# First self-attention: attention weights turned by 32x32 block transposes and gathering DMAs instead of TensorE transposes, and ScalarE's rounding of weights moved in its queue

## The chip, the cores and the metric

The kernel runs on one core of one Trainium2 chip, in one launch. The metric is the device time of that core in microseconds. The core has four computing engines, each with a queue of its own that runs in order: TensorE (PE in the views; its weight loads are PEld), VectorE (DVE), ScalarE (ACT) and GpSimd (POOL). SyncE (SP) issues the DMAs. The engines wait for each other on counted semaphores.

## The reference

Two blocks of two layers each run on a sequence of 512 tokens with 1024 features. The change lies in the first block's attention, in both of its layers:

```python
# first block, per layer; h = rms_norm(x); p = h @ w_in
q = apply_rope(rms_norm(q, q_g)); k = apply_rope(rms_norm(k, k_g))   # 8 heads of 64
score = sum_h relu(iq_h . ik) * iw_h            # an index score for each query and key
_, idx = lax.top_k(score masked causally, 128)  # 128 keys for each query
s = q . k_sel * HEAD_DIM ** -0.5                # causal, only the selected keys
p = softmax(s); o = p @ v_sel
y_b = (o * silu(gate)) @ w_out_attn
merged = g0 * y_conv + g1 * y_b + g2 * y_pool;  x = x + merged @ w_o
```

The rest of the first block (a short convolution and a pooling branch) and the second block (attention, a Hyena convolution, gated linear attention, cross-attention, a feed-forward part) are projections of the same kind with work of their own between them.

## The kernel before

**Units and queues.** `order_of_work` writes one list of units (`plan`). Every engine walks the same list and does its part of each unit, so the list sets the order of all queues. In the first block three lists (main: attention; sel: the top-k bias; side: the other branches) are merged by a string of digits, `PICKS["one0"]` and `PICKS["one"]`, written out by hand: each digit names the list that gives the next unit.

**Projections.** Most units are projections ("weight units" below: `q`, `k`, `agate`, `gate`, `by`, `hy`, `xk` and so on). A weight block travels: SP loads it into one of three raw buffers (`WRAW`); ACT rounds it into one of three buffers `WSP` (the high part, `next_halves`, L1350); POOL subtracts to get the rest (the low part, L1732); PE multiplies with three matmuls for each 128 features (L942 to L944). A full unit is 24 matmuls of 512 columns, a `by` unit of the first block 12. ACT calls `next_halves` at the head of a weight unit, before that unit's own work, for the block two ahead; the call waits for the matmuls of the block that used the same `WSP` buffer, three before it.

**Attention of the first block.** Heads go in pairs (`c` = 0 to 3, `hh` = 0, 1) and queries in four tiles of 128 (`i`). Only keys up to the tile's end are used, so tile `i` has 128(i+1) keys.

- `sc`: PE writes the scores into banks S0 and S1 (L1111). DVE adds the bias, takes the maximum and writes the scores to `PA` in SBUF (L2110), ACT takes the exponential in place with its sum (L1538).
- `nrm`: DVE inverts the sum, ACT scales `PA` (L1549).
- `tr`: PE turns the weights, one 128x128 transpose for each block of keys (L1007 on `PA`), into banks T0 and T1. DVE copies head 0 out (L2148), ACT head 1 (L1557), into `PTA`.
- `pv`: PE multiplies `PTA` with the values (L1148) into bank O. `atty` and `split` gate and round the result.
- `qss`, `kbc`: PE sums squares for the norms of `q` and `k` (L1082, sixteen instructions with 2 columns each) and turns the factors.

**The second block already turns its weights otherwise:** DVE transposes blocks of 32x32 (`STREAM_TRANSPOSE`, L2132, `BLK<-PB`), and eight DMAs a half (L2740, `PTB<-BLK`) bring blocks of the same key residue together on the partitions.

**Names that the steps touch.** `fspec` (L1198) and `tokx` (L1581, `HX<-B`) are units of the Hyena part; `park` evicts a gate to `HYT` and to DRAM. `msq` (L1649) squares the memory for the cross-attention; `go` is the gate of the linear attention (`GS<-B`); `xk` projects the memory (`MN`).

Of the kernel before, what the change touches and what calls it, by code (L numbers as in the profile page):

```python
# [23 lines left out]
        "1211211222112211120001102121112222011121211112212212100000200000000000020002002000002000000000000020"  # L24
        "020000000200000200020002000002000"
# [3 lines left out]
        "2212121211121212121121200000112121212112121112112121221212000002000000002000002000020000020000000000"  # L29
        "00020020000000200002002000002000002000"  # L30
# [329 lines left out]
def order_of_work(steps):  # L360
# [41 lines left out]
    def block_one(l):  # L402
# [34 lines left out]
        main += qk(0)  # L437
        for c in range(4):
            nxt = qk(c + 1) if c < 3 else []
            for i in range(4):  # L440
                main.append(Unit("sc", "a", l, c, i, s=True))
                main += nxt[:2]
                nxt = nxt[2:]
                if i:
                    main.append(Unit("tr", "a", l, c, i - 1, t=True))
                main.append(Unit("nrm", "a", l, c, i))
            main += nxt
            main.append(proj("agate", l, c, src=H, w=[(*A, "agate", c)]))
            main.append(Unit("tr", "a", l, c, 3, t=True))
            main.append(Unit("pv", "a", l, c, o=True))  # L450
            main += [Unit("atty", l, c), Unit("split", "YB", A, c)]
# [203 lines left out]
def program(nc, ins, place, out, steps=8):  # L655
    ctx = ExitStack()
    with ctx:
# [22 lines left out]
        PA, PTA, RXA, GA = at(45, "PA", 4), at(49, "PTA", 8), at(57, "RXA", 4), at(62, "GA", 3)  # L680
# [246 lines left out]
        def tensor(e):  # L927
# [85 lines left out]
            for u in plan:  # L1013
# [81 lines left out]
                elif k == "sc":  # L1095
# [7 lines left out]
                    for hh in range(2):  # L1103
                        half = slice(64 * hh, 64 * hh + 64)
                        if ab == "a":
                            b = take((S0, S1)[hh], dve_done, ("smax", ab, l, c, i, hh))
# [5 lines left out]
                elif k == "tr":  # L1112
                    ab, l, c, i = a
                    nk = i + 1
                    for hh in range(2):
                        b = take((T0, T1)[hh], (dve_done, act_done)[hh], ("pt", ab, l, c, i, hh))
                        w.wait_ge(act_done, ("nrm", ab, l, c, i, hh))
                        p = PA[:, 2 * (i % 2) + hh, :]
                        turn(b, [p[:, 128 * j:128 * j + 128] for j in range(nk)], nk, ("tr", ab, l, c, i, hh))
# [18 lines left out]
                elif k == "pv":  # L1138
                    ab, l, c = a
                    b = take(O, dve_done, ("lo", "YB", ("a", l), c))  # L1140
                    w.wait_ge(dve_done, ("pt", ab, l, c, 3, 0))
                    w.wait_ge(act_done, ("pt", ab, l, c, 3, 1))
                    w.wait_ge(act_done, ("tok", "vtok", l, 3))
                    for j in range(4):
                        q0 = 128 * j
                        for hh in range(2):
                            v = VA4[:, j, 128 * c + 64 * hh:128 * c + 64 * hh + 64]
                            x = e.matmul(b[64 * hh:64 * hh + 64, q0:512], v, PTA[:, 4 * hh + j, q0:512], start=j == 0, stop=j == 3)  # L1148
# [190 lines left out]
        def scalar(e):  # L1339
# [40 lines left out]
            for u in plan:  # L1380
                k, a = u.kind, u.a
                if own[-1] != act_done.n:
                    w.value(act_done.sem, own[-1])
                    own.append(act_done.n)
                for g in range(len(u.w)):
                    if u.w0 + g:
                        next_halves(u.w0 + g + NSP - 1)
                if k == "nadd":
# [137 lines left out]
                elif k == "sc":  # L1526
                    ab, l, c, i = a
                    n = 128 * (i + 1) if ab == "a" else 512
                    m = SM[:, 6 + i, :]
                    load_table(ACT.Exp)  # L1530
                    w.wait_ge(dve_done, ("neg", ab, l, c, i))
                    if ab == "b" and (c or i > 1):
                        back = (c, i - 2) if i > 1 else (c - 1, i + 2)
                        w.wait_ge(dve_done, ("blocks", l, *back, 1))
                    for hh in range(2):
                        p = (PA if ab == "a" else PB)[:, 2 * (i % 2) + hh, 0:n]
                        s = p if ab == "a" else banks[score_bank(ab, i, hh)][:, :]
# [5 lines left out]
                elif k == "nrm":  # L1543
                    ab, l, c, i = a
                    n = 128 * (i + 1)
                    w.wait_ge(dve_done, ("rsum", ab, l, c, i))
                    for hh in range(2):
                        p = PA[:, 2 * (i % 2) + hh, 0:n]
                        e.activation(p, p, ACT.Copy, scale=SM[:, 6 + i, 6 + hh:7 + hh]).then_inc(  # L1549
                            *act_done.up(("nrm", ab, l, c, i, hh)))  # L1550
                elif k == "tr":
                    ab, l, c, i = a
                    nk = i + 1
                    if i == 0 and c:
                        w.wait_ge(mm_done, ("pv", ab, l, c - 1))
                    w.wait_ge(mm_done, ("tr", ab, l, c, i, 1))
                    e.activation(PTA[:, 4:4 + nk, 128 * i:128 * i + 128],  # L1557
                                 banks[T1][:, 0:128 * nk].rearrange("p (k q) -> p k q", q=128), ACT.Copy).then_inc(
                        *act_done.up(("pt", ab, l, c, i, 1)))
# [245 lines left out]
        def vector(e):  # L1805
# [80 lines left out]
            for u in plan:  # L1886
# [206 lines left out]
                elif k == "sc":  # L2093
                    ab, l, c, i = a
                    n = 128 * (i + 1) if ab == "a" else 512
                    m, q2 = SM[:, 6 + i, :], SM[:, 4 + c % 2, 2 * i:2 * i + 2]
                    if ab == "a":
# [3 lines left out]
                        if c or i > 1:  # L2101
                            back = (c, i - 2) if i > 1 else (c - 1, i + 2)
                            w.wait_ge(mm_done, ("tr", ab, l, *back, 1))
# [38 lines left out]
                elif k == "tr":  # L2142
                    ab, l, c, i = a
                    nk = i + 1
                    if i == 0 and c:
                        w.wait_ge(mm_done, ("pv", ab, l, c - 1))
                    w.wait_ge(mm_done, ("tr", ab, l, c, i, 0))
# [409 lines left out]
        def sync(e):  # L2557
# [58 lines left out]
            for n_unit, u in enumerate(plan):  # L2616
# [405 lines left out]
```

## Time and profile before

| | us |
|---|---|
| median of 3 runs | 3255.43 (3254.47 to 3259.03) |
| profiled execution | 3252.9, its span 3250.9 |
| PE busy | 3223.4 |
| DVE, ACT, POOL busy | 1613.1, 1292.0, 1570.8 |

The span runs from the first instruction to the last. A busy PE is not PE at its peak: ends of matmuls are modelled and overlap the next start, so what an instruction costs is read from the distance between starts. `PEclk` is the TensorE clock that was granted, as a share of 2.4 GHz (0.50 is 1.2 GHz).

### The profile page before, as it was taken

How to read it: one execution, taken by the hardware profiler on the slowest of the kernel's cores; microseconds unless marked ns; L12 is line 12 of the kernel's file. 1: busy time of each engine (PE TensorE's matmuls, PEld its weight loads, DVE VectorE, ACT ScalarE, POOL GpSimd, SP SyncE). 2: the span in 40 equal slices, each digit the busy share in tenths (PEclk: the TensorE clock that was granted, in tenths of full speed). 3: DMA queues.
4: the chain of work that ended last, by engine and by line, in shares of the span. 5: the costliest groups of instructions: out<-in, count | busy, mean ns of one | idle time of the engine just before them, and what ended most of it. 6: DMA issues, size and time to landing. Idle time of an engine off the chain costs nothing.

```text
span 3250.9 us, 40100 instructions
## 1 busy us (share of the span) xinstructions
PE 3223.4 (99%) x15156; PEld 2547.6 (78%) x15156; DVE 1613.1 (50%) x2736; ACT 1292.0 (40%) x1984; POOL 1570.8 (48%) x1224
## 2 busy tenths in 40 slices
PE   9999999999999999999999999999999999999999
PEld 7788778787877767767788888887676788888887
DVE  4566433546543678864555321227887455442020
ACT  4343643334464322454446322232235544642231
POOL 4554334545434563334463565646333446446473
PEclk9999999999999999999999999999999999999999
DMA  4323224323223523452353433334236235334332
GB/s 158 98 84 97 75 88 147 120 94 92 81 84 91 184 98 101 142 145 81 112 182 98 130 118 97 102 122 139 91 119 166 77 112 187 118 117 123 97 91 97
DMA packets 145976, 370.16 MB, mean 114 GB/s; under 512 B 18670, under 2 KB 35630, under 8 KB 145784
## 3 DMA queue, kind: packets, MB, share of 16 engines
q1 hardware_dynamic: 145784, 367.60, 37.0%
q8 instruction: 120, 1.97, 0.2%
q14 instruction: 72, 0.59, 0.1%
HBM read 316.02 MB, written 25.30 MB: 105 GB/s over the span
## 4 chain that ended last, share of the span: by engine, by line
PE 93%; DVE 4%; ACT 2%; issue 1%; POOL 1%; DMA 0%; SPq 0%; DVEq 0%; ACTq 0%
PE B L942 27%; PE B L944 27%; PE B L943 27%; PE B L1007 1%; PE B L1111 1%; PE B L1134 1%; PE B L1167 1%; PE B L1209 1%; PE B L1217 1%; PE B L1198 1%; POOL WSP L1732 1%; PE B L1082 1%; PE B L1073 1%; PE B L1148 1%; PE B L1203 0%
## 5 line engine op out<-in xcount | busy, mean ns | idle before, releaser
L1732 POOL TENSOR_TENSOR WSP<-WRAW,WSP 128x512 fp32r<-128x512 f32 x1036 | 1359.0, 1333 | 1469.9 <-ACT WSP L1350 1469.4
L942 PE MATMUL B<-H,WSP 128*128 128x512 f32 x2496 | 993.0, 398 | 7.7 <-POOL WSP L1732 7.7
L944 PE MATMUL B<-H,WSP 128*128 128x512 f32 x2496 | 972.6, 390 | 0.0
L943 PE MATMUL B<-H,WSP 128*128 128x512 f32 x2496 | 971.9, 389 | 0.0
L1350 ACT ACTIVATE WSP<-WRAW 128x1024 fp32r<-128x1024 f32 (+1 forms) x567 | 555.8, 984 | 669.3 <-PE B L944 528.7
L942 PEld LDWEIGHTS B<-H,WSP 128*128 128x128 f32 x2496 | 468.8, 188 | 127.6 <-issue 25.3
L943 PEld LDWEIGHTS B<-H,WSP 128*128 128x128 f32 x2496 | 469.0, 188 | 100.9 <-issue 6.9
L944 PEld LDWEIGHTS B<-H,WSP 128*128 128x128 f32 x2496 | 468.5, 188 | 99.0
L1815 DVE TENSOR_TENSOR B<-B,RN 128x512 f32<-128x512 f32 x194 | 134.8, 697 | 392.1 <-PE B L944 375.8
L942 PE MATMUL B<-YM,WSP 128*128 128x512 f32 x512 | 199.5, 390 | 0.0
L944 PE MATMUL B<-YM,WSP 128*128 128x512 f32 x512 | 199.2, 389 | 0.0
L943 PE MATMUL B<-YM,WSP 128*128 128x512 f32 x512 | 199.2, 389 | 0.0
L2554 DVE TENSOR_TENSOR XN<-B,XN 128x512 f32<-128x512 f32 x32 | 22.1, 692 | 295.6 <-PE B L944 295.6
L2546 DVE SCALAR_TENSOR_TENSOR MR<-B,RN 128x512 f32<-128x512 f32 x64 | 44.3, 692 | 249.4 <-PE B L944 249.3
L1803 POOL TENSOR_TENSOR MR<-MR 128x512 f32<-128x512 f32 x64 | 88.6, 1385 | 91.3 <-DVE MR L2546 91.3
L942 PEld LDWEIGHTS B<-YM,WSP 128*128 128x128 f32 x512 | 96.1, 188 | 21.4 <-DVE XN L2554 1.6
L944 PEld LDWEIGHTS B<-YM,WSP 128*128 128x128 f32 x512 | 96.1, 188 | 20.0
L943 PEld LDWEIGHTS B<-YM,WSP 128*128 128x128 f32 x512 | 96.1, 188 | 19.9
L1370 ACT ACTIVATE GA<-B 128x512 f32<-128x512 f32 x48 | 28.7, 598 | 200.9 <-DVE B L1815 200.9
L942 PE MATMUL B<-YAC,WSP 128*128 128x512 f32 x256 | 103.5, 404 | 0.0
L943 PE MATMUL B<-YAC,WSP 128*128 128x512 f32 x256 | 101.1, 395 | 0.0
L944 PE MATMUL B<-YAC,WSP 128*128 128x512 f32 x256 | 100.9, 394 | 0.0
(451 smaller groups left out, 4806.8 us busy)
## 6 DMA issues: line engine op xcount, KB each, us to landing
WRAW<-in_wb SPq DMA_DIRECT2D x318, 512.0 KB, 3.7
WRAW<-in_wa SPq DMA_DIRECT2D x153, 512.0 KB, 3.7
PTB<-BLK SPq DMA_DIRECT2D x128, 128.0 KB, 2.7
WRAW<-in_wa SPq DMA_DIRECT2D x50, 256.0 KB, 2.6
WRAW<-in_wb SPq DMA_DIRECT2D x48, 256.0 KB, 2.6
parked<-HYT SPq DMA_DIRECT2D x24, 256.0 KB, 2.1
QA<-RXA SPq DMA_DIRECT2D x64, 64.0 KB, 2.0
xs<-PA SPq DMA_DIRECT2D x16, 256.0 KB, 4.4
```

What stands on the lines that cost most here:

```text
L942: e.matmul(o, L[0], R[0], start=first, stop=False)
L943: e.matmul(o, L[0], R[1], start=False, stop=False)
L944: return e.matmul(o, L[1], R[0], start=False, stop=last)
L1007: x = e.transpose(b[:, 128 * i:128 * i + 128], src[i], eye)
L1073: e.matmul(b[:, 0:n], QA[half, c % 2, 128 * i:128 * i + 128], KA[half, 1, 0:n], start=True, stop=True).then_inc(*mm_done.up(("idx", l, c, ...
L1082: x = e.matmul(b[:, 8 * n + 2 * i:8 * n + 2 * i + 2], sq[:, 128 * i:128 * i + 128], pair[:, ::64], start=True, stop=True)
L1111: e.matmul(b[:, 0:n], q, kk, start=True, stop=True).then_inc(*mm_done.up(("sc", ab, l, c, i, hh)))
L1350: e.activation(WSP[:, i % NSP, 0, 0:n * cols], WRAW[:, i % NRAW, 0:n * cols], ACT.Copy).then_inc(*hi_done.up(i))
L1732: x = e.tensor_tensor(WSP[:, i % NSP, 1, c:c + CUT], WRAW[:, i % NRAW, c:c + CUT], WSP[:, i % NSP, 0, c:c + CUT].bitcast(fp32), ALU.subtract)
L1803: e.tensor_tensor(t, t, t, ALU.mult).then_inc(*pool_done.up((k, *a)))
L1815: e.tensor_tensor(pj(u)[:, :], pj(u)[:, :], RN[:, :], ALU.mult).then_inc(*dve_done.up(("scaled", u.pj)))
L2546: e.scalar_tensor_tensor(MR[:, c % 4, :], pj(u)[:, :], 0.0, RN[:, :], ALU.max, ALU.mult).then_inc(*dve_done.up(("pj", u.pj), (k, *a)))
```

## The change

The `tr` units of the first block go. ACT now writes the exponentials in blocks of 32 keys into `PA`, reading the scores from the PSUM bank in a permuted order, so that key 128j+4k+b lies in block b; DVE transposes these 32x32 blocks in place (`ablocks`); SP gathers them with eight DMAs for each half of the queries (`agather`) into `PTA`; `pv` reads `PTA` with strides. Scores of four tiles use four banks. The order around the attention is written anew, and both strings of digits with it (two of their lines are shown). Apart from that, in all stages, ACT's `next_halves` now stands right behind a weight unit's own work, for the block three ahead (not for `woa` units).

```diff
 PICKS = {
     "one0": (
-        "1211211222112211120001102121112222011121211112212212100000200000000000020002002000002000000000000020"
+        "1211211222112211120001100212111222201112121111221221210000000000000020000200000000000000000000200002"
...
-        for c in range(4):
-            nxt = qk(c + 1) if c < 3 else []
-            for i in range(4):
-                main.append(Unit("sc", "a", l, c, i, s=True))
-                main += nxt[:2]
-                nxt = nxt[2:]
-                if i:
-                    main.append(Unit("tr", "a", l, c, i - 1, t=True))
-                main.append(Unit("nrm", "a", l, c, i))
-            main += nxt
-            main.append(proj("agate", l, c, src=H, w=[(*A, "agate", c)]))
-            main.append(Unit("tr", "a", l, c, 3, t=True))
-            main.append(Unit("pv", "a", l, c, o=True))
-            main += [Unit("atty", l, c), Unit("split", "YB", A, c)]
+        nxt = qk(1)
+        main += qk(0) + [sc(0, 0), *nxt[:2], nrm(0, 0), sc(0, 1), *nxt[2:4], turned(0, 0), nrm(0, 1), sc(0, 2), *nxt[4:], turned(0, 1),
+                         Unit("agather", l, 0, 0), nrm(0, 2), sc(0, 3), turned(0, 2), nrm(0, 3), turned(0, 3), Unit("agather", l, 0, 1)]
+        for c in range(4):
+            nxt = qk(c + 2) if c < 2 else []
+            if c:
+                main += [Unit("agather", l, c, 0), sc(c, 2), sc(c, 3), nrm(c, 2), turned(c, 2), nrm(c, 3), turned(c, 3),
+                         Unit("agather", l, c, 1)]
+            main += nxt[:2] + [proj("agate", l, c, src=H, w=[(*A, "agate", c)])]
+            if c < 3:
+                main += [sc(c + 1, 0), sc(c + 1, 1), nrm(c + 1, 0), nrm(c + 1, 1), *nxt[2:], turned(c + 1, 0), turned(c + 1, 1)]
+            main += [Unit("pv", "a", l, c, o=True), Unit("atty", l, c), Unit("split", "YB", A, c)]
...
-            return (S0, S1)[hh] if ab == "a" else (S0, S1, T0, T1)[(2 * i + hh) % 4]
+            return (S0, S1, T0, T1)[(2 * i + hh) % 4]
+        def query_half(t, h, hh):
+            return t[:, 2 + 2 * hh:4 + 2 * hh, :].rearrange("p s x -> p (s x)") if h else t[:, hh, :]
+        def weights_tile(i, hh):
+            t = query_half(PA, i // 2, hh).rearrange("p (b j i k) -> p i b j k", b=4, i=2, k=32)
+            return t[:, i % 2, :, 0:i + 1, :]
...
-                    for j in range(4):
-                        q0 = 128 * j
-                        for hh in range(2):
-                            v = VA4[:, j, 128 * c + 64 * hh:128 * c + 64 * hh + 64]
-                            x = e.matmul(b[64 * hh:64 * hh + 64, q0:512], v, PTA[:, 4 * hh + j, q0:512], start=j == 0, stop=j == 3)
+                    for h in range(2):
+                        for j in range(2 * h + 2):
+                            i0 = max(2 * h, j)
+                            for hh in range(2):
+                                v = VA4[:, j, 128 * c + 64 * hh:128 * c + 64 * hh + 64]
+                                p = query_half(PTA, h, hh).rearrange("p (r j q) -> p j r q", r=4, j=2 * h + 2)[:, j, :, 32 * (i0 - 2 * h):64]
+                                o = b[64 * hh:64 * hh + 64, :].rearrange("p (i r q) -> p r i q", i=4, r=4)[:, :, i0:2 * h + 2, :]
+                                x = e.matmul(o, v, p, start=j == 0, stop=j == 2 * h + 1)
...
-            for u in plan:
+            begun = None
+            for behind, u in zip([None] + plan, plan):
...
+                if behind and behind.w and behind.kind != "woa":
+                    next_halves(behind.w0 + len(behind.w) + NSP - 1)
                 for g in range(len(u.w)):
-                    if u.w0 + g:
+                    if g or begun and begun.kind == "woa":
                         next_halves(u.w0 + g + NSP - 1)
+                begun = u if u.w else begun
...
-                            x = e.tensor_tensor_reduce(out=PA[:, 2 * (i % 2) + hh, 0:n], in0=b[:, 0:n], in1=bias, scale=1.0, scalar=NEG,
+                            x = e.tensor_tensor_reduce(out=b[:, 0:n], in0=b[:, 0:n], in1=bias, scale=1.0, scalar=NEG,
                                                        op0=ALU.add, op1=ALU.max, accum_out=m[:, hh:hh + 1])
...
-                    e.tensor_copy(PTA[:, 0:nk, 128 * i:128 * i + 128],
-                                  banks[T0][:, 0:128 * nk].rearrange("p (k q) -> p k q", q=128)).then_inc(
-                        *dve_done.up(("pt", ab, l, c, i, 0)))
+                elif k == "ablocks":
+                    l, c, i = a
+                    for hh in range(2):
+                        p = weights_tile(i, hh)
+                        w.wait_ge(act_done, ("nrm", "a", l, c, i, hh))
+                        e.transpose(p, p).then_inc(*dve_done.up(("ablocks", l, c, i, hh)))
...
+                elif k == "agather":
+                    l, c, half = a
+                    next_raw(coming[n_unit] + NRAW + half)
+                    if half == 0 and c:
+                        w.wait_ge(mm_done, ("pv", "a", l, c - 1))
+                    w.wait_ge(dve_done, ("ablocks", l, c, 2 * half + 1, 1))
+                    for hh in range(2):
+                        for q in range(4):
+                            n = 128 + 128 * half
+                            e.dma_start(query_half(PTA, half, hh)[:, n * q:n * q + n], query_half(PA, half, hh)[32 * q:32 * q + 32]).then_inc(
+                                *gathered[half].up((k, *a)))
```

The first place is PE's queue in the first layer, around the product of head pair 1 (`pv`, `B<-PTA,VA`): the rows in it other than projections. Before:

```order
L1148 MATMUL B<-PTA,VA 64x512 [waits s_act_done,s_dve_done]
L1148 MATMUL B<-PTA,VA 64x512
L1148 MATMUL B<-PTA,VA 64x384 x2
L1148 MATMUL B<-PTA,VA 64x256 x2
L1148 MATMUL B<-PTA,VA 64x128 x2
L1111 MATMUL B<-KA,QA 128x128 x2
...
L1111 MATMUL B<-KA,QA 128x256 [waits s_dve_done] x2
L1082 MATMUL B<-CST,RXA 128x2 [waits s_act_done]
L1082 MATMUL B<-CST,RXA 128x2 x3
...
L1007 MATMUL B<-CST,PA 128x128 [waits s_act_done] x2
L1111 MATMUL B<-KA,QA 128x384 [waits s_dve_done] x2
```

And in the changed kernel:

```order
L1158 MATMUL B<-PTA,VA 64x4x2x32 [waits s_gathered1,s_gathered0]
L1158 MATMUL B<-PTA,VA 64x4x2x32
L1158 MATMUL B<-PTA,VA 64x128 x2
L1158 MATMUL B<-PTA,VA 64x4x2x32 x6
L1158 MATMUL B<-PTA,VA 64x128 x2
L1126 MATMUL B<-KA,QA 128x384 x2
L1126 MATMUL B<-KA,QA 128x512 x2
...
L1126 MATMUL B<-KA,QA 128x128 [waits s_act_done] x2
L1126 MATMUL B<-KA,QA 128x256 [waits s_act_done] x2
L1097 MATMUL B<-CST,RXA 128x2 [waits s_act_done]
L1097 MATMUL B<-CST,RXA 128x2 x3
```

The transposes of `PA` are gone, two `sc` units stand side by side, the product has twelve matmuls in place of eight over the same columns, and waits for the gathers. Between the scores of tiles 2 and 3 and the product that needs their gathers stand five projections: four full ones and a `by`, or three full ones and two `by`.

The second place is ACT's queue in the second block, at the change from the linear attention to the memory (`MACC`, `KSQ` are `msq`; `WSP<-WRAW` is a rounding). Before:

```order
L1639 ACTIVATE SM<-SM,EPSC 128x8 [waits s_dve_done]
L1649 ACTIVATE MACC<-MT 128x512 [waits s_act_done]
L1649 ACTIVATE KSQ<-MT 128x512
L1649 ACTIVATE KSQ<-MT 128x512 [waits s_dve_done] x2
L1350 ACTIVATE WSP<-WRAW 128x1024 [waits s_raw1,s_act_done]
L1364 ACT_TABLE_LOAD
L1364 ACTIVATE GS<-B 128x512 [waits s_dve_done]
L1350 ACTIVATE WSP<-WRAW 128x1024 [waits s_mm_done,s_raw2,s_act_done]
```

And in the changed kernel:

```order
L1656 ACTIVATE KSQ<-MT 128x512
L1656 ACTIVATE KSQ<-MT 128x512 [waits s_dve_done] x2
L1374 ACT_TABLE_LOAD [waits s_dve_done]
L1374 ACTIVATE GS<-B 128x512 [waits s_act_done]
L1360 ACTIVATE WSP<-WRAW 128x1024 [waits s_mm_done,s_raw2,s_act_done]
L1383 ACTIVATE KSQ<-B 128x256 [waits s_mm_done]
```

The rounding with `s_raw1` has left this place: it now stands further up, ahead of the squares of `gout` and of all of `msplit` and `msq`. And the table load ahead of `GS<-B` now carries the wait for DVE that the activation behind it carried before; in the whole program 25 table loads do so, where 4 did.

## Rows read from the trace of the kernel before

**Rows 1.** The page, busy time of each engine

```profile
PE 3223.4 (99%) x15156; PEld 2547.6 (78%) x15156; DVE 1613.1 (50%) x2736; ACT 1292.0 (40%) x1984; POOL 1570.8 (48%) x1224
```

**Rows 2.** The page, chain that ended last

```profile
PE 93%; DVE 4%; ACT 2%; issue 1%; POOL 1%; DMA 0%; SPq 0%; DVEq 0%; ACTq 0%
```

**Rows 3.** All waits of PE: waited for, total us, times, longest

```profile
PE B L942 <- POOL WSP L1732: 14.7, 9, 5.5
PE B L1007 <- ACT PA L1549: 1.8, 2, 1.0
PE B L1007 <- DVE SM L2110: 1.7, 2, 0.9
```

**Rows 4.** Groups of PE, forms apart: the transposes of PA

```profile
L1007 PE MATMUL B<-CST,PA 128*128 128x128 f32 x160 | 24.5, 280 | 3.7 <-ACT PA L1549 1.8 <-DVE SM L2110 1.7 <-DVE MS L2166 0.2
```

**Rows 5.** Timeline of PE: start us, us, instruction; eight transposes

```profile
323.42 0.39 PE L944 MATMUL B<-H,WSP 128*128 128x512 f32 x1
323.65 1.14 PE L1007 MATMUL B<-CST,PA 128*128 128x128 f32 x8
324.54 0.47 PE L942 MATMUL B<-H,WSP 128*128 128x512 f32 x1
325.08 0.40 PE L944 MATMUL B<-H,WSP 128*128 128x512 f32 x1
```

**Rows 6.** Timeline of PE: one product pv, and what follows

```profile
330.20 2.37 PE L1148 MATMUL B<-PTA,VA 128*64 128x512 f32 x16
332.51 0.49 PE L1111 MATMUL B<-KA,QA 64*128 64x128 f32 x4
```

**Rows 7.** Windows of PE: busy (instructions), PEclk, DMA share, GB/s

```profile
346.80:350.30 3.50, 3.50 (x10) 0.51 0.50 95
940.70:944.20 3.50, 3.50 (x9) 0.52 0.71 193
1596.00:1603.00 7.00, 3.66 (x17) 0.51 0.15 40
```

**Rows 8.** Timeline of PE: three waits for a low part

```profile
1413.63 0.47 PE L942 MATMUL B<-H,WSP 128*128 128x512 f32 x1 [1.65 <-POOL WSP L1732]
...
1512.89 0.47 PE L942 MATMUL B<-H,WSP 128*128 128x512 f32 x1 [1.17 <-POOL WSP L1732]
...
1599.34 0.55 PE L942 MATMUL B<-MN,WSP 128*128 128x256 f32 x1 [5.46 <-POOL WSP L1732]
```

**Rows 9.** Timeline of ACT ahead of two of these waits

```profile
1407.77 1.28 ACT L1519 ACT_TABLE_LOAD   x1
...
1409.23 1.05 ACT L1350 ACTIVATE WSP<-WRAW 128x1024 fp32r<-128x1024 f32 x1
...
1595.60 1.04 ACT L1350 ACTIVATE WSP<-WRAW 128x1024 fp32r<-128x1024 f32 x1
...
1598.44 1.05 ACT L1350 ACTIVATE WSP<-WRAW 128x1024 fp32r<-128x1024 f32 x1
```

**Rows 10.** PA and BLK by instruction: duration ns min/median/max

```profile
L1538 ACT ACTIVATE PA<-PA,SM x64: 477/648/817, 185.0 to 987.1; 128x128 f32<-128x128 f32 x16, 128x256 f32<-128x256 f32 x16, 128x384 f32<-128x384 f32 x16, 128x512 f32<-128x512 f32 x16
L1549 ACT ACTIVATE PA<-PA,SM x64: 386/555/725, 196.7 to 989.0; 128x128 f32<-128x128 f32 x16, 128x256 f32<-128x256 f32 x16, 128x384 f32<-128x384 f32 x16, 128x512 f32<-128x512 f32 x16
...
L2740 SPq DMA_DIRECT2D PTB<-BLK x128: 543/607/1740, 1353.5 to 2516.6; - x128
L2132 DVE STREAM_TRANSPOSE BLK<-PB x64: 664/686/712, 1350.1 to 2511.4; 128x512 f32<-128x512 f32 x64
...
DMA to landing us min/median/max: 2.5/2.7/3.8
```

**Rows 11.** Timeline of ACT, then of PE, at the unit tokx

```profile
1208.43 0.60 ACT L1370 ACTIVATE HYT<-B 128x512 f32<-128x512 f32 x1 [3.56 <-DVE B L1815]
1209.07 2.06 ACT L1581 ACTIVATE HX<-B 128x512 f32<-128x512 f32 x4
...
1210.28 3.60 PE L1198 MATMUL B<-HR,DF 128*128 128x512 f32 x8
```

More of the change, by code:

```diff
@@ L28 @@
         "0200002002000202022000200220022002012200000110121020200011221212000011211121121122220202202102012121"
-        "2212121211121212121121200000112121212112121112112121221212000002000000002000002000020000020000000000"
-        "00020020000000200002002000002000002000"
+        "2212121211121212121121200000011212121211212111211212122121200000000000000200002000000000000000000002"
+        "0000200000000000000200202020000000000002222000"
     ),
@@ L679, in program @@
         BIAS, VA4, QA, KA = at(34, "BIAS", 3), at(37, "VA4", 4), at(41, "QA", 2), at(43, "KA", 2)
-        PA, PTA, RXA, GA = at(45, "PA", 4), at(49, "PTA", 8), at(57, "RXA", 4), at(62, "GA", 3)
+        PA, PTA, RXA, GA = at(45, "PA", 6), at(51, "PTA", 6), at(57, "RXA", 4), at(62, "GA", 3)
         HR, HY = (at(0, "HR0", 8), at(16, "HR1", 8)), at(16, "HY", 8)
@@ L1105, in tensor @@
                         if ab == "a":
-                            b = take((S0, S1)[hh], dve_done, ("smax", ab, l, c, i, hh))
+                            b = take(score_bank(ab, i, hh), act_done, ("exp", ab, l, c, i, hh))
                             q, kk = QA[half, c % 2, 128 * i:128 * i + 128], KA[half, c % 2, 0:n]
@@ L1111, in tensor @@
                         e.matmul(b[:, 0:n], q, kk, start=True, stop=True).then_inc(*mm_done.up(("sc", ab, l, c, i, hh)))
-                elif k == "tr":
-                    ab, l, c, i = a
-                    nk = i + 1
-                    for hh in range(2):
[L1116 to L1119, printed above, removed]
                 elif k == "pbc":
@@ L1140, in tensor @@
                     b = take(O, dve_done, ("lo", "YB", ("a", l), c))
-                    w.wait_ge(dve_done, ("pt", ab, l, c, 3, 0))
-                    w.wait_ge(act_done, ("pt", ab, l, c, 3, 1))
+                    for h in range(2):
+                        w.wait_ge(gathered[h], ("agather", l, c, h))
                     w.wait_ge(act_done, ("tok", "vtok", l, 3))
-                    for j in range(4):
-                        q0 = 128 * j
-                        for hh in range(2):
-                            v = VA4[:, j, 128 * c + 64 * hh:128 * c + 64 * hh + 64]
-                            x = e.matmul(b[64 * hh:64 * hh + 64, q0:512], v, PTA[:, 4 * hh + j, q0:512], start=j == 0, stop=j == 3)
+                    for h in range(2):
+                        for j in range(2 * h + 2):
[5 more added lines that the diff above has]
+                                x = e.matmul(o, v, p, start=j == 0, stop=j == 2 * h + 1)
                     x.then_inc(*mm_done.up(("pv", *a)))
@@ L1531, in scalar @@
                     w.wait_ge(dve_done, ("neg", ab, l, c, i))
+                    if ab == "a" and c:
+                        w.wait_ge(gathered[i // 2], ("agather", l, c - 1, i // 2))
                     if ab == "b" and (c or i > 1):
@@ L1535, in scalar @@
                     for hh in range(2):
-                        p = (PA if ab == "a" else PB)[:, 2 * (i % 2) + hh, 0:n]
-                        s = p if ab == "a" else banks[score_bank(ab, i, hh)][:, :]
+                        p = weights_tile(i, hh) if ab == "a" else PB[:, 2 * (i % 2) + hh, :]
+                        s = banks[score_bank(ab, i, hh)][:, :]
+                        if ab == "a":
+                            s = s[:, 0:128 * (i + 1)].rearrange("p (j k b) -> p b j k", k=32, b=4)
                         e.activation(p, s, ACT.Exp, bias=m[:, 2 + hh:3 + hh], scale=SM[:, 4 + c % 2, 2 * i + hh:2 * i + hh + 1],
@@ L1544, in scalar @@
                     ab, l, c, i = a
-                    n = 128 * (i + 1)
                     w.wait_ge(dve_done, ("rsum", ab, l, c, i))
                     for hh in range(2):
-                        p = PA[:, 2 * (i % 2) + hh, 0:n]
+                        p = weights_tile(i, hh)
                         e.activation(p, p, ACT.Copy, scale=SM[:, 6 + i, 6 + hh:7 + hh]).then_inc(
                             *act_done.up(("nrm", ab, l, c, i, hh)))
[L1551 to L1559, printed above, removed]
                 elif k in ("fm1", "fm2"):
@@ L2096, in vector @@
                     m, q2 = SM[:, 6 + i, :], SM[:, 4 + c % 2, 2 * i:2 * i + 2]
+                    if (ab, c, i) == ("a", 0, 0):
+                        for x in range(8 if l else 0):
+                            w.wait_ge(landed, ("xs", 1, x))
+                        for h, t in enumerate((PA[:, 0:2, :], PA[:, 2:6, :])):
+                            ahead = t.rearrange("p s x -> p (s x)").rearrange("p (n j x) -> p j n x", n=8, j=2 + 2 * h)
+                            e.memset(ahead[:, 1 + 2 * h, :, 0:32], 0.0).then_inc(*dve_done.up(("ahead", l, h)))
                     if ab == "a":
```

20 lines of the change are left out of this document (8 added, 12 removed).

## The prediction

> **What bounds the kernel now.** I read the page's busy line first: TensorE is busy for 3223.4 us of a span of 3250.9, the three other engines for half of theirs or less [rows 1]. The chain that ended last says the same: 93% of it is PE, and no other engine has more than 4% [rows 2]. So time moves only when PE's queue gets shorter, when PE waits less, or when its clock changes; work on DVE, ACT, POOL or SP counts only where PE waits for it. Next, PE's waits: nine of them, 14.7 us in all, are for the low part of a weight block, and four more, 1.8 and 1.7 us, are at the transposes of `PA` [rows 3]. The timeline shows three of the nine with their lengths, 1.65, 1.17 and 5.46 us [rows 8]. Last, windows over stretches where PE's work looked thin show PEclk at 0.51 and 0.52 in place of full speed [rows 7].
>
> **The transposes.** The change takes away 160 of them, 24.5 us busy [rows 4]. Busy time overstates them, as their ends overlap. In the timeline eight stand between 323.65 and the next full matmul at 324.54, which is 0.89 us; the matmul behind them then reaches its successor only 0.54 us later (two full ones stand 0.23 apart ahead of them) [rows 5]. Some of that is wait rather than work, so I take 0.09 of it: 0.98 us for eight, 0.12 each. 160 times that is 19. In other places a few overlap better, so I take **-18.5**; the ends are -17.5 and, by busy time, -24.5. With them go PE's waits for ACT's scaling and for DVE at these instructions, **-3.5** [rows 3].
>
> **The product.** `pv` had 16 matmuls (eight in each of two halves of the array), 2.31 us from its start to the next instruction [rows 6]. It now has 24, over the same columns. Small matmuls cost nearly by their columns, so I take **0**. The upper bound from this side is one transpose for each of the 64 added instructions, 64 x 0.12 = +8. The other end is that a write in runs of 32 columns, strided over the bank, is slower: if it took twice as long, 8 x 2.3 = +18. No row of before has such a write, so this end is a rival below. The Trainium skill, "SBUF — State Buffer", section "Door 1: The DMA port swizzle", says that any non-contiguous PSUM access pattern significantly slows down matmuls; by it the sum below would lose up to those 18 us. No row before tests it; I give it a small chance, because the runs are 32 columns long and only their starts are strided.
>
> **What stands in for the transposes.** DVE: 64 block transposes of at most 0.69 us, less 32 copies. ACT: 32 copies less. SP: 128 more issues of 0.61 us each, 78 us in all [rows 10]. None is near PE's 99%. What matters is when `PTA` arrives. From the last scores of tile 3, one pair of tiles needs four exponentials of at most 0.82 us, four scalings of 0.73, four block transposes of 0.69, and DVE's reductions, for the first of which I take a transpose's 0.7 as an estimate: 3.3 + 2.9 + 2.8 + 0.7 = 9.7. Then eight issues of 0.61 (4.9) and a landing of 2.7: 17.3 us [rows 10]. The cover is the five projections between: a full unit is 24 matmuls of 0.227, 5.4 us (the step is that of [rows 5]), a `by` half, 2.7. Three full and two `by` give 21.8, four full and one `by` 24.5. So the gathers land 4 to 7 us ahead of `pv`: cost **0**. The slack is thin in this respect: ACT's queue now has a rounding (1.05 us) [rows 9] right behind each unit, ahead of exponentials, and where that rounding waits for its raw buffer, everything of the chain stands behind it. A landing can take 3.8 us, an issue 1.7 [rows 10]. SP issues two weight loads ahead of each set of gathers, so the raw buffers are filled first.
>
> **The clock.** Two stretches of 3.5 us run at half clock, each in the first block behind a stretch of thin work (scores, `qss`, transposes) [rows 7]. With the transposes gone PE comes to full columns sooner. If both go, each gives half its length, 1.7: **-3.4**. If `sc`, `sc` and `qss`, now side by side, thin the stretch as much, nothing.
>
> **Roundings moved.** The wait at 1413.63 follows a rounding that started at 1409.23, late because a table load and other work stood ahead of it [rows 8, 9]. Behind the unit that frees the slot it starts some microseconds earlier, so this 1.65 goes, and so does its like in the second layer (one of the remaining six of the nine, taken as long): -3.3. The wait of 1.17 at 1512.89 goes likewise: -1.2. The one of 5.46 us has two roundings ahead of it, 1595.60 and 1598.44 [rows 9]. The first moves far up, ahead of `msq`; the second now stands behind the gate `GS`, whose table load (1.28) waits for DVE. So the wait does not vanish: I take 2.5 off it, and half a microsecond off the half-clock stretch 1596 to 1603 [rows 7]: -3.0. Together **-7.5**; ends 0 and, if all 14.7 go and 3.5 of slow clock, -18.
>
> **What the move costs.** At `tokx` ACT's queue has `HYT<-B`, then four copies `HX<-B` that free banks for `fspec`, which starts 1.2 us behind the copies' start [rows 11]. Now the table load waits for DVE, so its 1.28 no longer hides in the 3.56 of idle time ahead of `HYT` [rows 9, 11], and a rounding of 1.05 stands ahead of the copies: they end 2.3 us later, at about 1213.4. `fspec` needs its next bank half-way, near 1212.1, and the third copy rather than the fourth: about 1 us of wait in each layer, **+2**. Ends 0 and 2 x 2.3 = +4.6.
>
> **Sum.** -18.5 - 3.5 + 0 - 3.4 - 7.5 + 2 = -30.9. The profiled execution took 3252.9, its span of 3250.9 and 2.0 around it, so after the change 3222.0. The median of the runs shown is 2.5 above the profiled one: 3224.5, and I write **3225**.
>
> **Rivals.** What follows are medians, 3255.4 plus each sum; 0.2% of it, 6.5 us, is about what a measurement of this kernel can tell from no change.
>
> *A, the forecast:* transposes, their waits, the slow stretches and half of the low-part waits go. 3218 to 3230.
>
> *B, the transposes alone:* -22, with clock and roundings giving nothing. The waits for POOL only change places, since ACT has as much to do as before at the same points and the string of digits puts units elsewhere. For it: the first of the two roundings at 1595.60 was early enough, and still PE waited [rows 8, 9]. 3233.
>
> *C, the strided product:* as A, but `pv` at double time, +18: 3243. For it: nothing in the rows; against it: the columns are the same and their runs long.
>
> *D, everything goes:* all 14.7 of the low-part waits, the half clock behind them, and no new wait at `fspec`: -18.5 - 3.5 - 3.4 - 18 = -43.4: 3212.
>
> *E, slower, the gathers arrive late:* the chain of 17.3 us becomes longer than its cover. It decides at 21.8 us for two head pairs and 24.5 for the other two. The place is the wait of `pv` for `gathered`. To eat the gain of 31 in eight products, each must wait 3.9 us; to be slower by 0.2%, 4.7, so a chain of 27 to 29 us. That takes ACT's queue held for 9 to 11 us in every pair, for example by a rounding that waits for a raw buffer not yet loaded. Then the time is 3262 and more, 3270 with the clock falling after such waits as it did after the 5.46 us one [rows 7, 8].
>
> *F, no change:* a part of E, 2 to 4 us a product, on average: 3249 to 3262.
>
> **How the numbers follow.** A 0.55; B 0.18; C 0.07; D 0.08; F 0.05; E 0.07. Likeliest is A, so 3225; its own range is 3218 to 3230. The range that holds 8 in 10 takes in B with its spread (-22 against the +4.6 and +8 of the bounds gives 3246 at the far end, most of it below 3240) and the edge of D: 3213 to 3240, leaving out the far half of D, C, and E and F. Faster by over 0.2% means below 3249: A, B, C, D, 0.88. Within 0.2%: F, 0.05. Slower: E, 0.07.
>
> **What would show it.** Transposes: no PE row on `PA`, PE's instruction count down by 160 less 64, busy time down by some 20. Product: eight groups of 24 at 2.3 us from start to next instruction; C shows as 4 us or more. Gathers: PE's waits for `PTB`-like landings on `PTA` of 0 to 1 us; E shows as several microseconds at each `pv`, with ACT or SP ahead of it in the chain. Clock: windows over the stretches of `sc`, `sc`, `qss` and the 4 us behind them, at 1.0 if right. Roundings: no wait of over 1 us for a low part near the memory of the convolution in either layer, about 3 us left at the first matmul on `MN`. New cost: a wait of PE for ACT inside `fspec`, near 1 us. The prediction is wrong by more than its range if waits stand at `pv`, if the clock falls in new places, or if the new order makes PE wait for scores or banks that the old one did not.

## The result, and the profile after

The changed kernel takes 3335.26 us (median of 4 runs, 3327.0 to 3339.2), against 3254.95 for the kernel before (4 runs, 3253.15 to 3259.03). The ratio is 1.0242, with a 95% interval of 1.0219 to 1.0264: 80 us slower, where 31 faster was forecast. The profiled run is the fastest of the four, 3327.0 with a span of 3325.2. One run of the kernel before, beside three of the experiments below, took 5153.48 us at a mean granted clock of 0.584, and is left out everywhere.

The page's busy line answers to [rows 1]:

```profile
PE 3235.3 (97%) x15060; PEld 2551.1 (77%) x15060; DVE 1672.7 (50%) x2772; ACT 1272.9 (38%) x1948; POOL 1592.2 (48%) x1224
```

PE issues 96 instructions fewer (160 transposes less, 64 matmuls more) and is nevertheless busy for 11.9 us longer. What PE is not busy has gone from 27.5 us (3250.9 less 3223.4) to 89.9. So five sixths of the 74.3 us by which the span has grown are waits. The rest is PE's busy time, which rose although PE has less to do: its mean granted clock is 0.990 in place of 0.998. By my estimate that costs some 26 us (0.008 of 3235.3), and the transposes that are gone hide about half of it. PE's waits by what was waited for (us in total, times, longest) answer to [rows 3]:

```profile
PE B L957 <- POOL WSP L1739: 25.2, 19, 3.2
PE B L1022 <- DVE RXA L1847: 23.5, 5, 6.9
PE B L957 <- DVE H L1905: 8.1, 7, 1.4
PE B L1097 <- ACT SM L1538: 6.9, 2, 3.5
PE B L1208 <- ACT HV L1588: 4.7, 2, 2.5
PE B L1263 <- ACT ES L1635: 4.6, 2, 2.3
PE B L1022 <- ACT GS L1374: 2.2, 1, 2.2
...
PE B L1208 <- ACT HX L1588: 1.3, 2, 0.7
```

No wait stands at the product `pv` (L1158) and none for a gather. Apart from some of the waits for the low part, only the second row lies in the new attention, and what PE waits for there is not the turned weights but `RXA`, the factor for the norm of `k`. The waits for `H`, `SM`, `HV`, `ES` and `GS` lie in parts of the program whose units did not change; only ACT's roundings moved there. The waits for the low part have grown from nine to nineteen.

ACT's own waits ahead of its roundings have changed as well. For raw blocks it stood 121.2 us in 45 waits before (53.4 and 67.8 us in these two rows); now it is 241.3 us in 72:

```profile
  DMA WRAW<-in_wa: 137.7, 35
  DMA WRAW<-in_wb: 103.6, 37
```

The timeline of PE shows one wait in the attention, and three at the norm behind the first layer:

```profile
354.06 1.09 PE L1022 MATMUL B<-CST,RXA 128*128 128x128 f32 x4 [6.60 <-DVE RXA L1847]
...
571.14 0.47 PE L957 MATMUL B<-H,WSP 128*128 128x512 f32 x1 [2.13 <-POOL WSP L1739]
...
576.70 0.50 PE L957 MATMUL B<-H,WSP 128*128 128x512 f32 x1 [1.23 <-DVE H L1905]
...
579.04 0.50 PE L957 MATMUL B<-H,WSP 128*128 128x512 f32 x1 [1.37 <-DVE H L1905]
```

Windows over three stretches (PE busy and its instructions, PEclk, DMA share, GB/s) answer to [rows 7]. The wait for `RXA` begins in the first window, at 347.5, still at full speed, and ends in the second; another lies in the third. In these two PEclk is 0.66, a mean of part at 0.5 and part at full speed:

```profile
340.00:350.00 10.00, 7.47 (x42) 1.00 0.53 178
350.00:360.00 10.00, 5.94 (x20) 0.66 0.14 52
390.00:400.00 10.00, 4.55 (x13) 0.66 0.19 52
```

**Why RXA is late.** Around 345 us ACT stands at a rounding, and its work for the attention stands behind it:

```profile
340.02 0.60 ACT L1374 ACTIVATE GA<-B 128x512 f32<-128x512 f32 x1 [2.44 <-DVE B L1822]
345.52 1.06 ACT L1360 ACTIVATE WSP<-WRAW 128x1024 fp32r<-128x1024 f32 x1 [4.90 <-DMA WRAW<-in_wa]
346.60 1.28 ACT L1367 ACT_TABLE_LOAD   x1
...
348.00 0.44 ACT L1555 ACTIVATE PA<-B,SM 128x128 f32<-128x128 f32 x1
...
351.46 1.28 ACT L1533 ACT_TABLE_LOAD   x1
352.75 0.27 ACT L1533 ACTIVATE SM<-B,EPSC 128x16 f32<-128x16 f32 x1
```

`GA<-B` is the own work of `agate`. Directly behind it stands the moved rounding, which waits 4.90 us for its raw block. PE had ended the scores for the exponentials at 340.04, and VectorE its part of them at 341.66. The `SM<-B` at the end feeds `RXA`. SP's queue says why the raw block was late:

```profile
330.72 5.13 SPq L2744 DMA_DIRECT2D PTA<-PA  x8
335.96 2.49 SPq L2570 DMA_DIRECT2D QA<-RXA  x4
338.55 2.91 SPq L2570 DMA_DIRECT2D KA<-RXA  x4
341.50 1.55 SPq L2584 DMA_DIRECT2D WRAW<-in_wa  x3
```

Eight gathers and eight rotations are issued one behind the other, and only then the next three raw blocks. The first of them is asked for at 341.50, and the rounding starts 4.0 us later.

**Why the norms are late.** In the stretch in which the first block's result is normed, SP saves and loads tiles of the residual (`xs`, `PA`). ACT's queue and SP's, in the kernel after:

```profile
1114.42 1.06 ACT L1360 ACTIVATE WSP<-WRAW 128x1024 fp32r<-128x1024 f32 x1 [5.07 <-issue]
1115.39 0.70 ACT L1406 ACTIVATE H<-PA,PAR 128x512 fp32r<-128x512 f32 x1
...
1122.35 1.06 ACT L1360 ACTIVATE WSP<-WRAW 128x1024 fp32r<-128x1024 f32 x1 [5.74 <-issue]
```

```profile
1110.00 0.43 SPq L2584 DMA_DIRECT2D WRAW<-in_wa  x1
...
1117.43 0.32 SPq L2570 DMA_DIRECT2D PA<-xs  x1
1117.80 0.43 SPq L2584 DMA_DIRECT2D WRAW<-in_wa  x1
```

This is a ring: a raw block is asked for at 1110.00; its rounding starts 4.4 us later, at 1114.42; behind it ACT makes `H`; DVE's part of `H` ends at 1117.40; SP's load `PA<-xs` waited for that; behind it, at 1117.80, stands the next raw block, and its rounding comes at 1122.35. One turn is 7.8 to 7.9 us, where a full unit of PE takes 5.4. The timeline names no cause for these two roundings (it says "issue"). But one turn earlier, where a block was asked for at 1100.34 and its rounding started at 1104.77, it names the DMA of the raw block, and the distance from the ask to the rounding is the same 4.4 to 4.6 us each time. In the kernel before roundings stood as far behind their asks, but the same rounding came one tile of the norm later in ACT's order, so that SP's next load did not wait for work behind it; roundings came 5.2 to 5.8 us apart there.

### The profile page after: what moved, and what is told of

The parts are those of the page before. It is cut to its first block and busy times, and to the rows that moved or that the text cites. A ratio compares the mean times of both kernels' runs of the same rounds, so it can differ in the third digit from the quotient of the medians.

```text
span 3325.2 us, 40059 instructions
## 1 busy us (share of the span) xinstructions
PE 3235.3 (97%) x15060; PEld 2551.1 (77%) x15060; DVE 1672.7 (50%) x2772; ACT 1272.9 (38%) x1948; POOL 1592.2 (48%) x1224
## 5 line engine op out<-in xcount | busy, mean ns | idle before, releaser
L1739 POOL TENSOR_TENSOR WSP<-WRAW,WSP 128x512 fp32r<-128x512 f32 x1036 | 1402.1, 1375 | 1490.9 <-ACT WSP L1360 1490.2
L1810 POOL TENSOR_TENSOR MR<-MR 128x512 f32<-128x512 f32 x64 | 67.5, 1054 | 99.5 <-DVE MR L2553 97.7
```

The costliest lines, as they stand in the source:

```text
L1739: x = e.tensor_tensor(WSP[:, i % NSP, 1, c:c + CUT], WRAW[:, i % NRAW, c:c + CUT], WSP[:, i % NSP, 0, c:c + CUT].bitcast(fp32), ALU.subtract)
L1810: e.tensor_tensor(t, t, t, ALU.mult).then_inc(*pool_done.up((k, *a)))
```

## The experiments

The ratios are against runs of the kernel before beside each experiment; its medians there were 3254.12 (move_alone, attention_alone, early_asks), 3255.09 (hybrid, att_asks, hybrid_asks, before_four), 3257.34 (after_agate, asks_agate, move_asks) and 3257.25 us (twice).

**move_alone** is the kernel before with ACT's roundings moved and nothing else. **attention_alone** is the changed kernel with them back. Their difference from the one and the other kernel is this piece:

```diff
-                for g in range(len(u.w)):
-                    if u.w0 + g:
-                        next_halves(u.w0 + g + NSP - 1)
+                if behind and behind.w and behind.kind != "woa":
+                    next_halves(behind.w0 + len(behind.w) + NSP - 1)
+                for g in range(len(u.w)):
+                    if g or begun and begun.kind == "woa":
+                        next_halves(u.w0 + g + NSP - 1)
```

> The kernel before, with ScalarE's roundings moved behind the weight units and nothing else of the change. Theory 1 (the loss comes from the moved roundings: each now stands ahead of other ScalarE work and waits for a raw buffer that SP has not asked for in time): 3300 to 3330 us, with PE's new waits outside the attention, in the hyena, norm and memory stretches, as in the changed kernel. Theory 2 (the loss comes from the new attention, its gathers on SP's queue and what they push back): 3245 to 3260, as before or a little faster.

Measured: 3333.47 us, ratio 1.0244 (1.0226 to 1.0263). That is 3.5 us above the range of theory 1 and far from theory 2: the loss was even larger than theory 1 had it. PE's waits for `H`, `SM`, `ES` and `HV` are those of the changed kernel to within 0.5 us:

```profile
PE B L942 <- POOL WSP L1736: 19.1, 15, 4.5
PE B L1007 <- ACT PA L1553: 11.9, 7, 3.5
PE B L942 <- DVE H L1902: 8.3, 7, 1.4
PE B L1082 <- ACT SM L1528: 6.9, 2, 3.6
PE B L1253 <- ACT ES L1632: 4.6, 2, 2.3
PE B L1198 <- ACT HV L1585: 4.2, 2, 2.2
```

> The changed kernel with the roundings back at the head of the next weight unit: transposes by blocks and gathers, and the new order, alone. Theory 1: 3230 to 3248 us, the gain of the removed transposes less a part for the new order's waits; the waits of 6 to 7 us for RXA ahead of the key factors shrink to under 2 us. Theory 2: 3310 or more, with the waits for RXA as they are.

Measured: 3259.74 us, ratio 1.0014 (1.0006 to 1.0023). Theory 2 falls, but theory 1's figure was too good as well: the attention alone is not 7 to 25 us faster, it is 5 slower (2 to 7). The waits for `RXA` are down to 1.9 us in all. In their place stand waits for the low part:

```profile
PE B L957 <- POOL WSP L1735: 30.4, 18, 5.5
PE B L1022 <- DVE RXA L1843: 1.9, 3, 0.7
```

Three of the new ones take 3.56 us each. One, and ACT ahead of it (timeline, then PE's first matmul behind the wait):

```profile
359.69 0.77 ACT L1551 ACTIVATE PA<-B,SM 128x512 f32<-128x512 f32 x1
...
362.33 1.34 ACT L1561 ACTIVATE PA<-PA,SM 128x512 f32<-128x512 f32 x2 [0.78 <-DVE SM L2129]
363.58 1.04 ACT L1360 ACTIVATE WSP<-WRAW 128x1024 fp32r<-128x1024 f32 x1
...
367.33 0.77 PE L957 MATMUL B<-H,WSP 128*128 128x512 f32 x1 [3.56 <-POOL WSP L1735]
```

Here the opposite is wrong: the rounding stands behind the exponentials and scalings of two tiles, which the new order put side by side.

**early_asks** is the changed kernel; SP asks for the raw block of the following weight unit ahead of its own waits:

```diff
                 for g in range(len(u.w)):
                     next_raw(u.w0 + g + NRAW)
+                if k in ("xld", "q", "k", "iq", "park", "hy", "agather") or k == "nadd" and a[0]:
+                    next_raw(coming[n_unit] + len(u.w) + NRAW)
```

> The changed kernel; SP asks for the raw weight block of the following weight unit ahead of its own waits at loads, rotations, parks and gathers. Theory 1, if it is the raw buffer that the moved rounding waits for: at least half of the loss comes back, 3295 us or less, and the period of 7.9 us of the units that write xs at the end of the first block falls toward 5.4. A rival within it (the rounding waits for the unit's matmuls, and ScalarE's other work is late for that): no change, 3327 to 3340.

Measured: 3267.56 us, ratio 1.0040 (1.0026 to 1.0053). Of 80 us, 68 (66 by the ratios) come back from SP's order alone, with ACT's queue untouched. ACT's waits for raw blocks fall from 241.3 us to 89.0, in 30 waits. So it is the raw block that most moved roundings wait for. The ring opens; roundings in the same stretch:

```profile
1098.44 1.05 ACT L1360 ACTIVATE WSP<-WRAW 128x1024 fp32r<-128x1024 f32 x1
...
1103.43 1.06 ACT L1360 ACTIVATE WSP<-WRAW 128x1024 fp32r<-128x1024 f32 x1 [2.81 <-DMA WRAW<-in_wa]
...
1110.18 1.06 ACT L1360 ACTIVATE WSP<-WRAW 128x1024 fp32r<-128x1024 f32 x1 [4.56 <-DMA WRAW<-in_wb]
...
1116.37 1.06 ACT L1360 ACTIVATE WSP<-WRAW 128x1024 fp32r<-128x1024 f32 x1 [3.99 <-DMA WRAW<-in_wb]
```

They are 5.0 to 6.8 us apart. Of PE's waits, 19.2 us for `RXA` remain. The edit does little at that place: the eight gathers and four of the rotations still stand ahead of SP's first ask, which comes at 339.56 in place of 341.50, and the rounding starts at 345.17 in place of 345.52.

**move_asks** is move_alone with the same edit of SP's asks.

> move_alone (the attention of before, all roundings moved) with SP asking for raw blocks ahead of its waits. Theory 1: most of the 79 us comes back, 3250 to 3275, and the waits around the norms at the ends of the blocks go (the first unit behind a norm, 11 us in place of 5.4, falls to 6.5). Rival (moved roundings cost by waiting for their unit's matmuls): over 3310.

Measured: 3265.76 us, ratio 1.0023 (1.0014 to 1.0033). The cure gives back as much with the old attention, 68 us, so it does not need the new gathers. The waits for the low part fall from 19.1 to 1.5 us, and those for `H` from 8.3 to 2.3. SP's early asks were not tried on the kernel before itself; the nearest run is att_asks below, where they are worth 4 us.

**after_agate** and **asks_agate** leave four roundings at the head of the next weight unit, those behind `agate` of pairs 0 and 1, in the changed kernel and in early_asks:

```diff
+            def held_back(v):
+                return v.kind == "woa" or v.kind == "agate" and v.a[1] < 2
...
-                if behind and behind.w and behind.kind != "woa":
+                if behind and behind.w and not held_back(behind):
...
-                    if g or begun and begun.kind == "woa":
+                    if g or begun and held_back(begun):
```

> The changed kernel; only behind agate of the pairs 0 and 1 the rounding stays at the head of the next weight unit (four roundings in all). Theory 1, refined (that rounding waits for its raw buffer ahead of exponentials, scalings and the factor for RXA): the four waits of 4.5 to 6.9 us for RXA go, with their slow clock, 3300 to 3315 us. Rival (RXA is late because the scores of two tiles side by side put too much on ScalarE and VectorE): the waits stay above 4 us, 3327 to 3340.

Measured: 3315.2 us, ratio 1.0176 (1.0161 to 1.0191), 0.2 us above what was expected. The four waits are gone (what is left for `RXA` is 3.1 us in five waits), so the rival falls. Part of the gain went to the low part, 25.2 to 30.7 us:

```profile
PE B L957 <- POOL WSP L1742: 30.7, 21, 4.7
...
PE B L1022 <- DVE RXA L1850: 3.1, 5, 0.8
```

> early_asks with the same four roundings left at the head of the next weight unit. If the two causes add up: 3236 to 3248 us. If curing one hides the other: 3255 to 3268.

Measured: 3251.72 us, ratio 0.9981 (0.9972 to 0.9991), between the two expectations. The four roundings are worth 16 us here by the medians and 19 by the ratios, against 20 and 21 without the asks, so the two causes add up for the most part.

**before_four** is the kernel before with four roundings of the second block moved, those for `EARLY`; **hybrid** is attention_alone with these and four of the first block. In both, ACT's loop is

```diff
+EARLY = (("agate", 0, 1), ("agate", 1, 1), ("gate", "a", 0, 2, 6), ("gate", "a", 1, 0, 6),
+         ("gate", "b", 0, 1, 7), ("gate", "b", 1, 1, 7), ("go", 0, 0, 0), ("xk", 0, 0, 1))
...
+                if behind and behind.w and behind.w0 + NSP in early:
+                    next_halves(behind.w0 + NSP)
                 for g in range(len(u.w)):
-                    if u.w0 + g:
+                    if u.w0 + g and u.w0 + g + NSP - 1 not in early:
                         next_halves(u.w0 + g + NSP - 1)
```

with the second line of names alone in before_four.

> The kernel before with four roundings moved behind their unit, those of the second block in hybrid (the seventh gates in both layers, go, the second xk); this is the part of the move from which the prediction took its gain of 7.5 us. Theory 1: 3246 to 3252 us, 3 to 8 us faster than before. Rival (the wait only goes to the next block): no difference, 3252 to 3257.

Measured: 3246.68 us, ratio 0.9975 (0.9966 to 0.9984), 8.4 us faster. The waits for the low part fall from 14.7 us [rows 3] to 3.6; a wait for `GS` comes up instead, and it is shorter than the 5.46 us one:

```profile
PE B L943 <- POOL WSP L1736: 3.6, 4, 1.1
...
PE B L1008 <- ACT GS L1365: 2.2, 1, 2.2
```

> attention_alone with eight of the roundings moved behind their unit, no others: the four in the first block whose weights PE waited for with ScalarE's attention work ahead of the rounding (agate of pair 1 in both layers, the gates 0,2,6 of layer 0 and 1,0,6 of layer 1), and four in the second block (the seventh gates, go, the second xk). Theory 1, refined (where exponentials stand ahead of a rounding it must go first; where its raw buffer is late it must not): the four waits of 3.6 us and their slow clock go, about 5 to 6 us each, and about 6 us in the second block: 3226 to 3240 us. Rival (the waits of attention_alone come from raw buffers that the gathers hold up on SP's queue, whatever ScalarE's order): 3250 to 3262.

Measured: 3237.91 us, ratio 0.9951 (0.9938 to 0.9963): 17 us faster than the kernel before and some 21 faster than attention_alone. As by theory 1. One wait of 3.58 us in the second layer stays.

> attention_alone with SP asking for the following raw weight block ahead of its own waits, as in early_asks. Theory 1, refined: the roundings stand behind exponentials and scalings, so earlier raw data change little: 3250 to 3262 us, and the waits of 3.6 us stay. Rival: 3230 to 3245, the waits of 3.6 us gone.

att_asks is attention_alone with the asks. Measured: 3255.48 us, ratio 1.0003 (0.9994 to 1.0012). The rival falls: two of its waits for the low part in the attention are still 3.6 us, a third is 2.8. Where roundings stand behind exponentials, earlier raw data are worth 4 us.

> hybrid with the early asks too. Theory 1, refined: within 5 us of hybrid. Rival (raw buffers): 10 us or more faster than hybrid.

hybrid_asks is hybrid with the asks. Measured: 3232.16 us, ratio 0.9932 (0.9917 to 0.9947), the fastest kernel of the study, 23 us faster than the kernel before. Its 5.8 us against hybrid lie between the two expectations and decide nothing. Its waits for the low part are half of those of hybrid:

```profile
PE B L959 <- POOL WSP L1740: 6.4, 7, 1.9
```

**twice** is the kernel before with every transpose of `PA` made twice:

```diff
+                        for j in range(nk):
+                            e.transpose(b[:, 128 * j:128 * j + 128], p[:, 128 * j:128 * j + 128], eye)
                         turn(b, [p[:, 128 * j:128 * j + 128] for j in range(nk)], nk, ("tr", ab, l, c, i, hh))
```

> The kernel before with each of the 160 transposes of PA made twice into the same place, nothing else: the price of what the change removed. By the prediction's working (0.12 us each, 18.5 in all) 3272 to 3277 us; by busy time (24.5) 3279 or more; if transposes mostly hide in waits that PE has at these places, under 3268.

Measured: 3268.83 us, ratio 1.0037 (1.0025 to 1.0049), so 160 transposes cost 8 to 16 us, best 12, which is 0.05 to 0.10 us each. The time itself lies between the expected ranges. They were reckoned from some 3254, while the kernel before took 3257.25 beside this run, so the difference counts: 12 us, where the working had 18 and the busy time 24.5. The interval takes in the 14 below which transposes were said to hide mostly, so it neither bears that out nor excludes it.

The profiles show hardly any such hiding. The profiled execution of twice, the slowest of its six, has a span 19.4 us longer than that of the kernel before, PE's busy time is 19.7 us longer (3223.4 to 3243.1), and what PE is not busy stays the same (27.5 and 27.2). The waits at the transposes, 3.5 us before [rows 3], are 1.8 now, at the added set, which comes first (L1120):

```profile
PE B L1120 <- ACT PA L1551: 1.8, 4, 0.5
```

Part of the 19.4 us is the clock, as executions of one kernel differ in it. Beside this run the two of the kernel before with a mean granted clock of 0.998 in the record had spans of 3249.2 and 3251.6, and the three of twice with the same clock 3264.4 to 3265.8. At equal clock the 160 transposes cost about 15 us, 0.09 each, which lies within the interval.

## Why the prediction was wrong

**The step that failed** is "Roundings moved". The prediction put it as "Behind the unit that frees the slot it starts some microseconds earlier", took 7.5 us of gain from it, and set its ends at 0 and -18. Measured alone (move_alone), it costs 79 us, nearly all of the result. The mechanism that it described is real where it was looked at: before_four moves the roundings of the waits that it priced, the like in the second layer with them, and gains 8.4, against the 7.5. But the change moves the roundings of nearly all 568 weight blocks, and apart from `tokx` I priced only places where PE waited before. At the others the rounding had nothing to gain, as PE did not wait, and something to lose: it has two conditions, the slot and the raw block, and the step looked at the slot alone. Where SP asks late, the rounding now holds the work behind it on ACT. The runs show it in four ways: ACT's waits for raw blocks doubled (121.2 to 241.3 us), the loss is there without the new attention (move_alone), SP's asks alone give 68 us of it back (early_asks, and again move_asks), and four roundings alone are worth 20 us (after_agate).

**The order on ACT was the place to look**, and the prediction had half of it. It said that a rounding which waits for its raw block would hold everything behind it, but it tied this to the gathers and dismissed it: "SP issues two weight loads ahead of each set of gathers, so the raw buffers are filled first". After those gathers SP issues eight rotations before it asks again, and one of the roundings behind them waits for just that ask. Rival E had the right sign and the right mechanism on ACT, but its place was `pv`. In no kernel did PE wait for `gathered`. What it waited for was the factor `RXA`, behind the same exponentials.

**The transposes** went as forecast in kind. The size of -18.5 was too large: doubling them costs 8 to 16, about 15 at equal clock. In hybrid, whose mean granted clock is that of the kernel before (0.998), PE's busy time is 15.4 us shorter (3223.4 to 3208.0). The price per transpose was read from one stretch in which eight followed each other between full matmuls, and it was high. The 3.5 us of waits at them did go, but hybrid has 2.7 us of waits for `PA` at the scores, where there were none.

**The product** costs nothing, as taken. In attention_alone all eight take 2.31 or 2.32 us from start to next instruction, as in [rows 6]. One of them:

```profile
348.58 2.38 PE L1158 MATMUL B<-PTA,VA 128*64 128x256 f32 x24
350.89 1.77 PE L1126 MATMUL B<-KA,QA 64*128 64x384 f32 x8
```

Rival C is out. The rule of the Trainium skill that stood beside it ("SBUF — State Buffer", "Door 1: The DMA port swizzle": non-contiguous PSUM patterns slow matmuls significantly) does not show here, with runs of 32 columns; the measurement decides.

**The clock** term has the wrong sign. Of windows of 10 us in the first block, attention_alone has six with PEclk under 0.97, where the kernel before has two (0.84 and 0.83). Two of its waits of 3.56 us are followed by

```profile
367.30:377.00 9.70, 9.67 (x47) 7.70 (x47) 2.25 (x11) 4.34 (x6) 3.74 (x3) 0.83 0.65 153
412.20:420.00 7.80, 7.77 (x22) 6.16 (x23) 0.00 (x0) 1.06 (x1) 3.62 (x3) 0.61 0.52 168
```

(length; busy time and instructions of PE, PEld, DVE, ACT and POOL; PEclk; DMA share; GB/s). By my estimate from these rows, PE lost some 3.0 us at a PEclk of 0.61 over 7.8 us (0.39 of 7.8), and some 1.6 at 0.83 over 9.7. So one wait cost nearly as much again, and the other half as much again. hybrid still has five windows under 0.97; no run tried their cause.

**The cost at `fspec`** was taken as 2 us. The two waits for `HX`, which it was taken for, are 1.3 us in all in the changed kernel: right. But two waits for `HV`, 4.7 us in all, are new at the same line (L1208) and had no term. With early_asks those for `HV` go and those for `HX` stay, so the raw blocks made the former.

**Sum of attention_alone.** Forecast, without the roundings: -18.5 - 3.5 - 3.4 = -25. Measured: +5. PE's busy time fell by 8.1 us (3223.4 to 3215.3), which is the transposes less the slower clock (0.995 in place of 0.998). The waits rose by 17.5 (27.5 to 45.0), of which 15.7 are for the low part (14.7 to 30.4). The prediction had no term for them. I had taken it that the new order of units left the roundings of the attention where they were, but the exponentials of two tiles now stand ahead of one rounding. hybrid, with eight roundings in front, gives 17 us of gain. Of the forecast 31, hybrid_asks reaches 23. No run tried the new order of units without the gathers, so how the cost of attention_alone divides between them is known only by the places of its waits: none stands at a gather.

## What to carry to other kernels

A call that prefetches on an in-order queue has two sides: who waits for its result, and what stands behind it while it waits for its input. Move it ahead only where its consumer waited and its input is surely there, and price the move at every place that it touches, not only at the stalls that it is meant for. When such a call moves, look at the queue that issues its load too: here a load asked for ahead of that queue's own waits gave back 68 of 80 us.

## What the hardware showed that I had not expected

- A product written in runs of 32 columns, strided over its bank, in 24 matmuls in place of 16, takes the same 2.31 us as the contiguous one, at all eight places.
- 160 additional transposes of 128x128 cost 12 us (8 to 16), about 15 at equal clock, where their own durations add up to 44 us (0.27 each).
- From SP's issue of a raw block of 512 KB to ACT's rounding of it passed 4.4 to 4.6 us in each turn of the ring, where the page of the profile gives a median of 3.9 from issue to landing.
